# Turns by ordinary products, and the recurrence's transfers in quarters, in a two-block kernel on one core

## The chip, the cores and the metric

The kernel runs on one core of one Trainium2 chip. The metric is the device time of one execution in microseconds (us). Three timed runs of the kernel before gave 2231.57, 2232.23 and 2235.17 us, median 2232.23.

## The reference, cut to what matters

Two transformer blocks run one after the other on x of 256 tokens by 2048 channels, in float32: first windowed attention with a pooling branch and a gated feed-forward, then an RWKV-7 mixer followed by differential attention. The change lies in the RWKV-7 mixer of the second block. Its recurrence, with 32 heads of 64 channels:

```python
def step(S, inp):
    r_t, w_t, k_t, v_t, kk_t, a_t = inp
    sa = jnp.einsum('bhvk,bhk->bhv', S, kk_t)
    S = (S * w_t[:, :, None, :]
         - sa[..., None] * (kk_t * a_t)[:, :, None, :]
         + v_t[..., None] * k_t[:, :, None, :])
    y = jnp.einsum('bhvk,bhk->bhv', S, r_t)
    return S, y
...
mu = jnp.mean(y, -1, keepdims=True)
yc = y - mu
var = jnp.mean(yc * yc, -1, keepdims=True)
y = (yc * lax.rsqrt(var + GN_EPS)).reshape(B, T, C) * gn_g + gn_b
bonus = jnp.sum(rh * kh * r_k, -1, keepdims=True) * vh
y = (y + bonus.reshape(B, T, C)).astype(x.dtype)
return (y * jax.nn.silu(g)) @ w_out
```

## The kernel before, in words

Most of the time goes to large weight products. A unit of weights is 512 KB; SyncE loads it (`raw_w`), ScalarE makes its high part (`w_hi`), VectorE the low part (`w_lo`), and TensorE multiplies. All instructions stand in an order written out by hand, engine by engine, and semaphores tie the engines together.

The recurrence (called WKV here) is done in chunks of 64 tokens: `STEPS` has 16 steps n = (group g of 8 heads, chunk c), four steps to a group, and from 1505 to 1624 us the program does little else. In step n TensorE does, in this order: `x_second` (the state's part of X), `k_pairs(n + 1)`, a product with the inverse (`u_done` rises to 2n + 1), `turn_v(n + 1)`, the cross product, `beta_pairs(n + 1)`, the state's part of the output, the second product with the inverse (`u_done` 2n + 2), `turn_k(n + 1)`, the product that updates the state, `turn_beta(n + 1)`, `x_first(n + 1)` and the output (`y_done` n + 1). Between them ScalarE and VectorE copy what the next product needs: `XS` (L1898), `US` (L1902), the second copies of U (ScalarE L1908, VectorE L2575), K and beta turned (L1880), the state's two steps (L2587, L2589, or L2593 alone when c is 0). The turns of k and beta belong to steps whose next step has c < 3; where the step itself has c = 3 there is no state update, and `x_first` comes ahead of `turn_beta`.

A turn brings a 128 x 64 tile into token order by the identity, four tiles at a time. `turn_v` (L1247) uses ordinary products that write partitions 0 to 63 and 64 to 127 in turns. `turn` (L1249 to L1256) uses a product (L1253) where the output lies in partitions 64 to 127 and TensorE's transpose mode (L1255) where it lies in 0 to 63. An ordinary float32 product shows as two instructions in the trace, a transpose as one.

SyncE issues every transfer. Before the steps it issues three `load_t` and the eight broadcasts of the bonus rows (`spread_bonus`, 256 KB each). Then, for each n from 3 on, it waits for `y_done` n - 2 and issues `load_t(n)` (the inverse blocks and cross blocks of step n, in eight small transfers, three buffers deep); at eight of these places `first_unit`, a 512 KB unit of the weights that follow; and at three of them `spread_rows`, which waits for a group's rsqrt rows, stores them, waits for the store and loads them back broadcast (`GWIDE`, two transfers of 256 KB). `head_pair` on VectorE uses `GWIDE` and the bonus; GpSimd multiplies the bonus by v (`times_v`). At c = 0 of groups 1 to 3 VectorE also makes the reciprocal of the variances (L2611), and in groups 2 and 3 a `head_pair` behind it. On ScalarE, steps 5, 9 and 13 end with a Sqrt of the rows (in step 5 behind a table load) and the split of a weight unit, ahead of the next step's `XS`.

Of the kernel before, what the change touches and what calls it, by code (L numbers as in the profile page):

```python
# [14 lines left out]
P = 128  # L15
T = 256
# [126 lines left out]
def program(nc, h):  # L143
# [14 lines left out]
    with root:  # L158
# [291 lines left out]
        lt_dram, t_dram, x_dram = dram("lt_scratch", (P, 3, H, H)), dram("t_scratch", (P, 2, H, H)), dram("x_scratch", (P, KD, T))  # L450
# [47 lines left out]
        def _(sp):  # L498
# [66 lines left out]
            def load_t(n):  # L565
                g, c = STEPS[n]
                m = n % 3
                src = t_dram.rearrange("(f c h) b s t -> c h b s f t", c=NCH, h=2)
                for hh in range(2):
                    for b in range(2):  # L570
                        at = 64 * hh + H * b
                        sp.dma_start(TB[at:at + H, m, :, H * b:H * b + H], src[c, hh, b, :, 4 * g:4 * g + 4, :])\
                          .then_inc(t_loaded[m], 16)
                cross = lt_dram.rearrange("(f c h) b s t -> c h b s f t", c=NCH, h=2)
                for e in range(2):
                    for h_ in range(2):
                        sp.dma_start(CRS[64 * (1 - e):64 * (1 - e) + H, m, 2 * h_:2 * h_ + 2, H:], cross[c, h_ ^ e, 2, :, 4 * g + e:4 * g + 4:2, :])\
                          .then_inc(t_loaded[m], 16)


            def store_lt(f):
                sp.wait_ge(lt_ready, f + 1)
                dst = lt_dram[8 * f:8 * f + 8].rearrange("(c h) b s t -> h b s c t", h=2)
                for hh in range(2):
                    for b in range(2):
                        at = 64 * hh + H * b
                        sp.dma_start(dst[hh ^ f % 2, b], (XS, US)[f % 2][at:at + H, :, H * b:H * b + H]).then_inc(lt_stored[f % 2], 16)
                    sp.dma_start(dst[hh ^ f % 2, 2], (XS, US)[f % 2][64 * hh:64 * hh + H, :, H:]).then_inc(lt_stored[f % 2], 16)
# [25 lines left out]
            for n in range(NW):  # L614
# [7 lines left out]
                if n == 71:  # L622
                    for even_odd in lt_stored:
                        sp.wait_ge(even_odd, 96 * KD // 2)
                    sp.dma_start(LT[:, :, :, :], lt_dram[:, 0:2]).then_inc(inv_in, 16)
# [12 lines left out]
            def first_unit(n, w):  # L638
                sp.wait_ge(unit_done, seen(unit_done))
                sp.dma_start(RAWW[:, n, :, :], w.rearrange("(k p) n -> p k n", p=P)[:, n // 2 * KU:(n // 2 + 1) * KU,  # L640
                                                                                   n % 2 * UNIT_COLS:(n % 2 + 1) * UNIT_COLS])\
                  .then_inc(landed[n], 16)

            def spread_bonus(g):

                for h_ in range(2):
                    sp.dma_start(BON[64 * h_:64 * h_ + 64, 4 * g:4 * g + 4, :], b_dram[2 * g + h_:2 * g + h_ + 1].broadcast_to([64, 4, T]))\
                      .then_inc(bon_in, 16)

            def spread_rows(g):  # L650

                sp.wait_ge(gn_rstd, g + 1)
                for i in range(4):
                    sp.dma_start(g_dram[g, :, i, :], GROWS[32 * i:32 * i + 2, 1, :]).then_inc(gn_stored, 16)
                sp.wait_ge(gn_stored, 64 * (g + 1))
                if g:
                    sp.wait_ge(gn_out, 2 * g)
                for h_ in range(2):
                    sp.dma_start(GWIDE[64 * h_:64 * h_ + 64, :, :], g_dram[g, h_:h_ + 1].broadcast_to([64, 4, T])).then_inc(gn_loaded, 16)
# [15 lines left out]
            sp.wait_ge(gn_loaded, 96)  # L675
# [23 lines left out]
        def _(pool):  # L699
# [45 lines left out]
            def times_v(g):  # L745
                pool.wait_ge(bon_in, 128)
# [8 lines left out]
            def step(n):  # L755
# [10 lines left out]
                if n in (3, 5, 7, 9):  # L766
                    times_v((n - 3) // 2)
# [16 lines left out]
        def _(pe):  # L784
# [521 lines left out]
            def step(n):  # L1306
# [9 lines left out]
                pe.wait_ge(t_loaded[n % 3], 128 * (n // 3 + 1))  # L1316
# [126 lines left out]
        def _(act):  # L1443
# [5 lines left out]
            def split_unit(u, ku=KU):  # L1449
                act.wait_ge(landed[u], seen(landed[u], 16))  # L1450
# [434 lines left out]
            def head_rstd(g):  # L1885
                act.wait_ge(gn_var, g + 1)
                if g:
                    act.wait_ge(gn_loaded, 32 * g)
# [6 lines left out]
            def step(n):  # L1895
# [18 lines left out]
                if n in SPLIT_AT:  # L1914
                    split_unit(SPLIT_AT.index(n))
# [10 lines left out]
            split_unit(4)  # L1926
            head_rstd(3)
            split_unit(5)
            split_unit(6)
            for p_ in (6, 7):  # L1930
                act.wait_ge(gn_gated, p_ + 1)
                act.activation(C4H[:, 2 * p_:2 * p_ + 2, :], BET[:, 2 * p_:2 * p_ + 2, :], ACT.Copy).then_inc(gn_hi, 1)
                if p_ == 6:
                    split_unit(7)
# [129 lines left out]
        def _(dve):  # L2064
# [502 lines left out]
            def step(n):  # L2567
# [37 lines left out]
                if c == 3 and 0 < g < 3:  # L2605
                    dve.wait_ge(gn_loaded, 32 * g)
# [32 lines left out]
            dve.wait_ge(gn_loaded, 96)  # L2639
# [248 lines left out]
```

## Time and profile before

| | |
|---|---|
| timed runs | 2231.57, 2232.23, 2235.17 us |
| profiled execution, own time | 2236.7 us |
| its span | 2234.9 us |
| granted TensorE clock, mean | 0.991 |
| busy: TensorE, its weight loads, VectorE, ScalarE, GpSimd | 98%, 83%, 67%, 48%, 4% |
| chain that ended last | TensorE 88%, VectorE 8%, ScalarE 2%, issue 2% |
| mean traffic | 172 GB/s |

The table says that TensorE sets the time nearly everywhere. Busy shares are means over stages, so what a change inside the recurrence is worth has to be read from that stretch: 1505 to 1624 us, where many small products follow one another through copies on the other engines. "Issue" is time in which an engine waited for nothing that the profile shows. A timeline row gives the start, the time from first start to last end of merged instructions, engine, line, operation and count, and in brackets the idle time before with its releaser.

### The profile page before, as it was taken

To read this page: it belongs to the slowest core of one execution; us is meant where nothing else is said; L and a number is where in the kernel's file an instruction comes from. 1 tells how busy PE (TensorE), PEld (TensorE's weight loads), DVE (VectorE), ACT (ScalarE), POOL (GpSimd) and SP (SyncE) were. 2 spreads that over 40 slices of the span, in tenths; PEclk is the share of its full clock that TensorE was granted. 3 is DMA by queue.
4 is the path that set the end of the run, shared out by engine and by line. 5 is a ranking of instruction groups with operands and counts; after the bars stand their busy time and mean duration, and the time that the engine had idled before them with its cause. 6 is when DMAs were issued, how large, how long until landed. Compare 5 with 4: busy or idle time off the path is not lost.

```text
span 2234.9 us, 38358 instructions
## 1 busy us (share of the span) xinstructions
PE 2183.0 (98%) x14672; PEld 1856.4 (83%) x14672; DVE 1486.2 (67%) x2054; ACT 1079.9 (48%) x1520; POOL 89.1 (4%) x78
## 2 busy tenths in 40 slices
PE   9999999999999999999899999998999999999997
PEld 7888888888888888888788888886688888888886
DVE  6656568885588856875884589764576644566655
ACT  5444564444444434445544756444434534456533
POOL 0700000000000000000000000001210000000000
PEclk9999999999999999999999999999999999999998
DMA  8654555665666666656465555652355555654562
GB/s 290 207 161 155 170 151 178 189 188 186 189 189 188 188 187 189 188 163 192 136 221 142 174 162 164 203 158 61 81 183 161 170 187 189 189 153 145 166 187 85
DMA packets 400097, 383.35 MB, mean 172 GB/s; under 512 B 44009, under 2 KB 397857, under 8 KB 399137
## 3 DMA queue, kind: packets, MB, share of 16 engines
q1 hardware_dynamic: 399970, 381.59, 55.5%
q8 instruction: 88, 1.44, 0.3%
q14 instruction: 39, 0.32, 0.0%
HBM read 374.65 MB, written 6.87 MB: 171 GB/s over the span
## 4 chain that ended last, share of the span: by engine, by line
PE 88%; DVE 8%; ACT 2%; issue 2%; DMA 1%; DVEq 0%; SPq 0%; ACTq 0%
PE acc L795 45%; PE acc L798 22%; PE acc L826 3%; PE acc L881 2%; PE acc L882 2%; PE acc L883 2%; PE aux L1167 2%; PE acc L829 2%; DVE w_lo L2076 2%; PE acc L1253 1%; ACT w_hi L1452 1%; PE aux L1076 1%; PE aux L898 1%; PE aux L1096 1%; PE acc L1255 0%
## 5 line engine op out<-in xcount | busy, mean ns | idle before, releaser
L2076 DVE TENSOR_TENSOR w_lo<-raw_w,w_hi 128x1024 fp32r<-128x1024 f32 (+1 forms) x592 | 712.9, 1224 | 456.4 <-ACT w_hi L1452 454.9
L1452 ACT ACTIVATE w_hi<-raw_w 128x1024 fp32r<-128x1024 f32 (+1 forms) x592 | 613.3, 1046 | 674.5 <-PE acc L798 575.0
L795 PE MATMUL acc<-h,w_hi 128*128 128x512 f32 x1664 | 525.8, 397 | 1.2 <-DVE w_lo L2076 1.2
L798 PEld LDWEIGHTS acc<-h,w_lo 128*128 128x128 f32 x1664 | 312.6, 188 | 73.8
L798 PE MATMUL acc<-h,w_lo 128*128 128x256 f32 x1664 | 327.0, 278 | 0.0
L795 PEld LDWEIGHTS acc<-h,w_hi 128*128 128x128 f32 x1664 | 254.5, 189 | 2.2 <-issue 1.4
L795 PE MATMUL acc<-x_split,w_hi 128*128 128x512 f32 x704 | 225.2, 401 | 0.0
L795 PE MATMUL acc<-ff,w_hi 128*128 128x512 f32 x704 | 221.7, 396 | 2.4 <-DVE ff L2333 2.4
L795 PE MATMUL acc<-xs_b,w_hi 128*128 128x512 f32 x512 | 162.5, 399 | 1.7 <-DVE w_lo L2521 0.9
L798 PEld LDWEIGHTS acc<-ff,w_lo 128*128 128x128 f32 x704 | 132.2, 188 | 31.2
L798 PEld LDWEIGHTS acc<-x_split,w_lo 128*128 128x128 f32 x704 | 132.2, 188 | 31.2
L795 PE MATMUL acc<-xs_a,w_hi 128*128 128x512 f32 x448 | 143.7, 402 | 3.2 <-DVE w_lo L2076 3.2
L2521 DVE TENSOR_TENSOR w_lo<-raw_w,w_hi 128x1024 fp32r<-128x1024 f32 x96 | 116.7, 1222 | 44.5 <-ACT w_hi L1831 43.2
L798 PE MATMUL acc<-x_split,w_lo 128*128 128x256 f32 x704 | 138.6, 278 | 0.0
L798 PE MATMUL acc<-ff,w_lo 128*128 128x256 f32 x704 | 138.3, 278 | 0.0
L1831 ACT ACTIVATE w_hi<-raw_w 128x1024 fp32r<-128x1024 f32 x96 | 100.5, 1053 | 54.9 <-PE acc L798 43.1
L798 PEld LDWEIGHTS acc<-xs_b,w_lo 128*128 128x128 f32 x512 | 96.2, 188 | 22.7
L795 PEld LDWEIGHTS acc<-x_split,w_hi 128*128 128x128 f32 x704 | 108.1, 189 | 4.1 <-issue 3.1
L795 PEld LDWEIGHTS acc<-ff,w_hi 128*128 128x128 f32 x704 | 107.1, 189 | 4.2 <-DVE ff L2333 2.0
L798 PEld LDWEIGHTS acc<-xs_a,w_lo 128*128 128x128 f32 x448 | 84.1, 188 | 19.9
L798 PE MATMUL acc<-xs_b,w_lo 128*128 128x256 f32 x512 | 100.7, 278 | 0.0
L1519 ACT ACTIVATE fold<-acc 128x512 f32<-128x512 f32 x128 | 74.7, 583 | 30.4 <-PE acc L798 20.5
(374 smaller groups left out, 3128.6 us busy)
## 6 DMA issues: line engine op xcount, KB each, us to landing
raw_w<-in_w_up SPq DMA_DIRECT2D x176, 512.0 KB, 3.5
raw_w<-in_a_w_in SPq DMA_DIRECT2D x128, 512.0 KB, 3.8
raw_w<-in_w_in SPq DMA_DIRECT2D x64, 512.0 KB, 4.0
raw_w<-in_w_down SPq DMA_DIRECT2D x64, 512.0 KB, 3.6
raw_w<-in_b_w_qg SPq DMA_DIRECT2D x64, 512.0 KB, 3.8
raw_w<-in_w_o SPq DMA_DIRECT2D x32, 512.0 KB, 3.6
raw_w<-in_a_w_out SPq DMA_DIRECT2D x32, 512.0 KB, 3.6
raw_w<-in_w_k_shared SPq DMA_DIRECT2D x32, 512.0 KB, 3.7
```

The source lines that it names most:

```text
L795: pe.matmul(ACC[2 * b + f], WHI[:, q, k, f * P:(f + 1) * P], op[:, kt, :, :].rearrange("p h t -> p (h t)"), start=first, stop=False)
L798: mm = pe.matmul(ACC[2 * b + f][:, 0:T], WLO[:, slot, k, f * P:(f + 1) * P], op[:, kt, 0, :], start=False, stop=last)
L826: pe.matmul(ACC[2 * b + f], WHI[:, (2 * x + b) % 4, k, f * P:(f + 1) * P], op[:, kt, :, :].rearrange("p h t -> p (h t)"), start=first, sto ...
L829: mm = pe.matmul(ACC[2 * b + f][:, 0:T], WLO[:, 2 * x + b, k, f * P:(f + 1) * P], op[:, kt, 0, :], start=False, stop=last)
L881: pe.matmul(out, xh, wh[:, :, k, :], start=(kt == 0), stop=False)
L882: pe.matmul(out, xh, wl[:, :, k, :], start=False, stop=False)
L883: mm = pe.matmul(out, xl, wh[:, :, k, :], start=False, stop=(kt == KD - 1))
L1452: act.activation(WHI[:, u % 4, 0:ku, :], RAWW[:, u, 0:ku, :], ACT.Copy).then_inc(hi_made, 1)
L1519: act.activation(FOLD[:, j0:j0 + 2, :], BANKS[:, j0:j0 + 2, T:], ACT.Copy, scale=scale).then_inc(low_half, 1)
L1831: act.activation(WHI[:, n % 4, :, :], RAWW[:, slot, :, :], ACT.Copy).then_inc(hi_made, 1)
L2076: dve.tensor_tensor(WLO[:, u, 0:ku, :], RAWW[:, u, 0:ku, :], WHI[:, u % 4, 0:ku, :].bitcast(F32), ALU.subtract)\
L2521: dve.tensor_tensor(WLO[:, slot_of(n), :, :], RAWW[:, slot_of(n), :, :], WHI[:, n % 4, :, :].bitcast(F32), ALU.subtract)\
```

## The change

All turns of k and beta become ordinary products, four in a row. SyncE's order in the recurrence is rewritten around three events of each step. Each step may carry one transfer of 512 KB (a weight unit, a bonus spread or the spread of the rsqrt rows), cut into four quarters of 128 KB: the first goes out when X of the step is done, the second and third at the two `u_done` events, the fourth behind `y_done` and `load_t`. The bonus broadcasts move from ahead of the steps into steps 0, 3, 5 and 8; the rows of groups 0 to 2 go in steps 6, 10 and 14; the weight units in the steps 1, 2, 4, 7, 9, 11, 12 and 13. The cross blocks get a scratch of their own (`cross_dram`), laid out so that `load_t` takes two transfers for them in place of four. GpSimd's `times_v` moves from steps 3, 5, 7, 9 to 2, 5, 7, 10. Counts of the semaphores follow.

```diff
+        cross_dram = dram("cross_scratch", (4, NCH, 2, H, 4, H))
...
-                for e in range(2):
-                    for h_ in range(2):
-                        sp.dma_start(CRS[64 * (1 - e):64 * (1 - e) + H, m, 2 * h_:2 * h_ + 2, H:], cross[c, h_ ^ e, 2, :, 4 * g + e:4 * g + 4:2, :])\
-                          .then_inc(t_loaded[m], 16)
+                for e in range(2):
+                    sp.dma_start(CRS[64 * (1 - e):64 * (1 - e) + H, m, :, H:], cross_dram[g, c, e]).then_inc(t_loaded[m], 16)
...
+            UNIT_AT, BONUS_AT, ROWS_AT = [1, 2, 4, 7, 9, 11, 12, 13], [0, 3, 5, 8], [6, 10, 14]
+            def unit_quarter(n, k):
+                if k == 0:
+                    sp.wait_ge(unit_done, seen(unit_done))
+                row, col = (n // 2 * KU + k) * P, n % 2 * UNIT_COLS
+                sp.dma_start(RAWW[:, n, k, :], h["a_w_out_2"][0, row:row + P, col:col + UNIT_COLS]).then_inc(landed[n], 16)
+            def bonus_quarter(g, k):
+                if k == 0 and g:
+                    sp.wait_ge(bon_in, 64 * g)
+                sp.dma_start(BON[32 * k:32 * k + 32, 4 * g:4 * g + 4, :], b_dram[2 * g + k // 2:2 * g + k // 2 + 1].broadcast_to([32, 4, T]))\
+                  .then_inc(bon_in, 16)
+            def rows_quarter(g, k):
+                if k == 0:
+                    sp.wait_ge(gn_rstd, g + 1)
+                    for i in range(4):
+                        sp.dma_start(g_dram[g, :, i, :], GROWS[32 * i:32 * i + 2, 1, :]).then_inc(gn_stored, 16)
+                    sp.wait_ge(gn_stored, 64 * (g + 1))
+                    if g:
+                        sp.wait_ge(gn_out, 2 * g)
+                sp.dma_start(GWIDE[32 * k:32 * k + 32, :, :], g_dram[g, k // 2:k // 2 + 1].broadcast_to([32, 4, T])).then_inc(gn_loaded, 16)
...
-            UNIT_AT = [4, 6, 8, 9, 10, 12, 13, 14]
-            for g in range(4):
-                spread_bonus(g)
-            for n in range(3, 4 * NCH):
-                sp.wait_ge(y_done, n - 2)
-                load_t(n)
-                if n in UNIT_AT:
-                    first_unit(UNIT_AT.index(n), h["a_w_out_2"][0])
-                if n >= 7 and n % 4 == 3:
-                    spread_rows(n // 4 - 1)
+            for s_ in range(4 * NCH):
+                sp.wait_ge(x_done, s_ + 1)
+                quarter(s_, 0)
+                sp.wait_ge(u_done, 2 * s_ + 1)
+                quarter(s_, 1)
+                sp.wait_ge(u_done, 2 * s_ + 2)
+                quarter(s_, 2)
+                if s_ + 3 < 4 * NCH:
+                    sp.wait_ge(y_done, s_ + 1)
+                    load_t(s_ + 3)
+                quarter(s_, 3)
...
-                if n in (3, 5, 7, 9):
-                    times_v((n - 3) // 2)
+                if n in (2, 5, 7, 10):
+                    times_v((2, 5, 7, 10).index(n))
...
             def turn(x, n, half):
                 for i in range(4):
-                    if half ^ i % 2:
-                        mm = pe.matmul(KB_BANK[64:P, i * P:(i + 1) * P], tile_of(x, n, i), IDENT, start=True, stop=True)
-                    else:
-                        mm = pe.transpose(KB_BANK[0:64, i * P:(i + 1) * P], tile_of(x, n, i), IDENT)
+                    b = half ^ i % 2
+                    mm = pe.matmul(KB_BANK[64 * b:64 * b + 64, i * P:(i + 1) * P], tile_of(x, n, i), IDENT, start=True, stop=True)
```

TensorE at steps 0 and 1, before. The names are the turned tile (`consts,x` is turn_v, `consts,k` turn_k, `consts,beta` turn_beta), `aux<-wkv_x,inverse_blocks` the product with the inverse, `acc<-wkv_small` the state's update.

```order
L1167 MATMUL aux<-wkv_x,inverse_blocks 64x64 x8
L1255 MATMUL acc<-consts,k 64x128
L1253 MATMUL acc<-consts,k 64x128
L1255 MATMUL acc<-consts,k 64x128
L1253 MATMUL acc<-consts,k 64x128
L1167 MATMUL acc<-wkv_small 64x64 x8
L1253 MATMUL acc<-consts,beta 64x128
L1255 MATMUL acc<-consts,beta 64x128
L1253 MATMUL acc<-consts,beta 64x128
L1255 MATMUL acc<-consts,beta 64x128
```

The same place now.

```order
L1256 MATMUL acc<-consts,x 64x128 x4
L1176 MATMUL aux<-wkv_u,cross_blocks 64x64 x8
L1243 MATMUL acc<-r_kappa,beta 64x64 x8
L1176 MATMUL aux<-wkv_x,inverse_blocks 64x64 x8
L1262 MATMUL acc<-consts,k 64x128 x4
L1176 MATMUL acc<-wkv_small 64x64 x8
L1262 MATMUL acc<-consts,beta 64x128 x4
```

Nothing changed place on TensorE; each turn is now one form of instruction, the one that turn_v (L1256 now) has.

SyncE's queue from the rows of group 0 to `load_t(10)` with the unit behind it, before. L654 stores the rsqrt rows, L659 spreads them, L572 and L577 are load_t, L640 the weight unit.

```order
L654 DMA head_rstd_scratch<-head_rstd_rows 2x256 x4
L659 DMA head_rstd_wide<-head_rstd_scratch 64x1024 x2
L572 DMA inverse_blocks<-t_scratch 32x4x32 x4
L577 DMA cross_blocks<-lt_scratch 32x2x32 x4
L640 DMA raw_w<-in_a_w_out 128x4x256
L572 DMA inverse_blocks<-t_scratch 32x4x32 x4
L577 DMA cross_blocks<-lt_scratch 32x2x32 x4
L640 DMA raw_w<-in_a_w_out 128x4x256
```

From the same rows, now in step 6 (L655 and L659), to `load_t(10)` and the unit's last quarter in step 7.

```order
L655 DMA head_rstd_scratch<-head_rstd_rows 2x256 x4
L659 DMA head_rstd_wide<-head_rstd_scratch 32x1024 x3
L573 DMA inverse_blocks<-t_scratch 32x4x32 x4
L576 DMA cross_blocks<-cross_scratch 32x4x32 x2
L659 DMA head_rstd_wide<-head_rstd_scratch 32x1024
L643 DMA raw_w<-in_a_w_out 128x256 x3
L573 DMA inverse_blocks<-t_scratch 32x4x32 x4
L576 DMA cross_blocks<-cross_scratch 32x4x32 x2
L643 DMA raw_w<-in_a_w_out 128x256
```

The rows' last quarter moved behind the six transfers of `load_t(9)`; `load_t(8)` no longer stands behind the rows; and the 512 KB in one piece are gone.

## Rows read from the trace of the kernel before

**Rows 1.** TensorE's timeline (start us, us, line, shapes, count), turns of step 5.
```profile
1544.49 0.66 PE L1247 MATMUL acc<-consts,x 128*64 128x128 f32 x8
1545.08 0.46 PE L1167 MATMUL aux<-wkv_u,cross_blocks 64*64 64x64 f32 x16
...
1546.09 0.46 PE L1167 MATMUL aux<-wkv_x,inverse_blocks 64*64 64x64 f32 x16
1546.48 0.30 PE L1255 MATMUL acc<-consts,k 128*64 128x128 f32 x1
1546.71 0.43 PE L1253 MATMUL acc<-consts,k 128*64 128x128 f32 x2
1547.07 0.30 PE L1255 MATMUL acc<-consts,k 128*64 128x128 f32 x1
...
1548.04 0.38 PE L1253 MATMUL acc<-consts,beta 128*64 128x128 f32 x2
...
1549.17 1.08 PE L1167 MATMUL aux<-wkv_small 64*64 64x64 f32 x32
```

**Rows 2.** TensorE's timeline, the same stretch of step 14, without turns.
```profile
1615.98 0.46 PE L1167 MATMUL aux<-wkv_x,inverse_blocks 64*64 64x64 f32 x16
1616.99 0.69 PE L1167 MATMUL acc<-wkv_small 128*64 128x64 f32 x16 [0.55 <-DVE wkv_small L2575]
1617.61 1.08 PE L1167 MATMUL aux<-wkv_small 64*64 64x64 f32 x32
```

**Rows 3.** TensorE's timeline, step 11 into step 12.
```profile
1594.45 0.46 PE L1167 MATMUL aux<-wkv_x,inverse_blocks 64*64 64x64 f32 x16
...
1597.60 0.69 PE L1167 MATMUL aux<-wkv_small 128*64 128x64 f32 x16
...
1598.72 0.46 PE L1167 MATMUL aux<-wkv_x,inverse_blocks 64*64 64x64 f32 x16
```

**Rows 4.** Timeline of step 8, VectorE and TensorE.
```profile
1575.71 0.42 DVE L2593 TENSOR_TENSOR wkv_s<-acc,chunk_decay 128x256 f32<-128x256 f32 x1 [0.47 <-PE acc L1167]
...
1579.23 0.88 DVE L2628 SCALAR_TENSOR_TENSOR beta<-beta,params,bonus 128x256 f32<-128x256 f32 x2
...
1580.50 0.46 PE L1234 MATMUL acc<-r_kappa,beta 64*64 64x64 f32 x16 [0.35 <-DVE wkv_small L2553]
```

**Rows 5.** Timeline of steps 6 to 8, TensorE and SyncE's queue.
```profile
1559.55 0.43 SPq L640 DMA_DIRECT2D raw_w<-in_a_w_out  x1
...
1561.91 0.46 PE L1167 MATMUL aux<-wkv_x,inverse_blocks 64*64 64x64 f32 x14
...
1564.83 0.37 PE L1167 MATMUL aux<-wkv_x,inverse_blocks 64*64 64x64 f32 x2 [2.46 <-issue]
...
1571.44 0.40 PE L1167 MATMUL aux<-wkv_x,inverse_blocks 64*64 64x64 f32 x16
```

**Rows 6.** DMA view, 1559 to 1564 us (packets, MB, share of 16 engines).
```profile
q8 instruction: 1, 0.02, 2.5%
...
raw_w<-in_a_w_out SPq DMA_DIRECT2D x1, 512.0 KB, 5.9
```

**Rows 7.** DMA view, whole execution.
```profile
q8 instruction: 88, 1.44, 0.3%
```

**Rows 8.** Windows: length, TensorE busy (instructions), granted clock, DMA share, GB/s.
```profile
1564.00:1565.00 1.00, 0.17 (x2) 0.71 0.18 34
...
1622.00:1623.00 1.00, 0.45 (x20) 0.72 0.97 410
```

**Rows 9.** Timeline of step 3: SyncE's queue, TensorE, VectorE.
```profile
1529.43 1.73 SPq L572 DMA_DIRECT2D inverse_blocks<-t_scratch  x4
...
1532.50 0.46 PE L1167 MATMUL aux<-wkv_x,inverse_blocks 64*64 64x64 f32 x16
...
1533.48 0.69 DVE L2559 TENSOR_TENSOR wkv_small<-acc,consts 128x512 f32<-128x512 f32 x1
```

**Rows 10.** Tile view of the rsqrt rows' scratch.
```profile
DMA to landing us min/median/max: 3.4/4.0/4.9
```

More of the change, by code:

```diff
@@ L449, in by_chunk @@
             return x.rearrange("p (c t) -> p c t", c=NCH)
-        lt_dram, t_dram, x_dram = dram("lt_scratch", (P, 3, H, H)), dram("t_scratch", (P, 2, H, H)), dram("x_scratch", (P, KD, T))
+        cross_dram = dram("cross_scratch", (4, NCH, 2, H, 4, H))
+        lt_dram, t_dram, x_dram = dram("lt_scratch", (P, 2, H, H)), dram("t_scratch", (P, 2, H, H)), dram("x_scratch", (P, KD, T))
         g_dram, b_dram = dram("head_rstd_scratch", (3, 2, 4, T)), dram("bonus_scratch", (8, 4, T))
@@ L624, in _ @@
                         sp.wait_ge(even_odd, 96 * KD // 2)
-                    sp.dma_start(LT[:, :, :, :], lt_dram[:, 0:2]).then_inc(inv_in, 16)
+                    sp.dma_start(LT[:, :, :, :], lt_dram).then_inc(inv_in, 16)
                 if n == 84:
@@ L636, in _ @@
                 load_t(n)
[L638 to L659, printed above, removed]
@@ new lines, in quarter @@
+            def quarter(s_, k):
+                if s_ in UNIT_AT:
+                    unit_quarter(UNIT_AT.index(s_), k)
+                if s_ in BONUS_AT:
+                    bonus_quarter(BONUS_AT.index(s_), k)
+                if s_ in ROWS_AT:
+                    rows_quarter(ROWS_AT.index(s_), k)
+            sp.wait_ge(bon_stored, 64)
+            for s_ in range(4 * NCH):
[9 more added lines that the diff above has]
+                quarter(s_, 3)
@@ L674, in _ @@
             sp.wait_ge(tok_done, v_turned(4 * NCH - 1))
-            sp.wait_ge(gn_loaded, 96)
+            sp.wait_ge(gn_loaded, 192)
             sp.wait_ge(bon_done, KD)
@@ L745, in times_v @@
             def times_v(g):
-                pool.wait_ge(bon_in, 128)
+                pool.wait_ge(bon_in, 64 * (g + 1))
                 b4 = BON[:, 4 * g:4 * g + 4, :]
@@ L1315, in step @@
                     k_pairs(n + 1)
-                pe.wait_ge(t_loaded[n % 3], 128 * (n // 3 + 1))
+                pe.wait_ge(t_loaded[n % 3], 96 * (n // 3 + 1))
                 pe.wait_ge(xs_ready, n + 1)
@@ L1447, in _, with split_unit @@
             seen(acc_free, 4, "tile")
-            def split_unit(u, ku=KU):
-                act.wait_ge(landed[u], seen(landed[u], 16))
+            def split_unit(u, ku=KU, transfers=1):
+                act.wait_ge(landed[u], seen(landed[u], 16 * transfers))
                 act.wait_ge(unit_done, seen(unit_done))
@@ L1887, in head_rstd @@
                 if g:
-                    act.wait_ge(gn_loaded, 32 * g)
+                    act.wait_ge(gn_loaded, 64 * g)
                 act.activation(GROWS[:, 1, :], GROWS[:, 0, :], ACT.Sqrt).then_inc(gn_rstd, 1)
@@ L1914, in step @@
                 if n in SPLIT_AT:
-                    split_unit(SPLIT_AT.index(n))
+                    split_unit(SPLIT_AT.index(n), transfers=4)
             v_copies(0)
@@ L1925, in _ @@
             operand_hi(2)
-            split_unit(4)
+            split_unit(4, transfers=4)
             head_rstd(3)
-            split_unit(5)
-            split_unit(6)
+            split_unit(5, transfers=4)
+            split_unit(6, transfers=4)
             for p_ in (6, 7):
@@ L1933, in _ @@
                 if p_ == 6:
-                    split_unit(7)
+                    split_unit(7, transfers=4)
             def post_norm_gemm(which, bufs, more):
@@ L2605, in step @@
                 if c == 3 and 0 < g < 3:
-                    dve.wait_ge(gn_loaded, 32 * g)
+                    dve.wait_ge(gn_loaded, 64 * g)
                     head_pair(2 * (g - 1), [GWIDE[:, k, :] for k in range(2)])
@@ L2638, in _ @@
             operand_lo(1)
-            dve.wait_ge(gn_loaded, 96)
+            dve.wait_ge(gn_loaded, 192)
             head_pair(4, [GWIDE[:, k, :] for k in range(2)])
```

3 lines of the change are left out of this document (1 added, 2 removed).

## Prediction, made before the changed kernel was run

> **What bounds the kernel now.** I read the page's busy shares and chain first. TensorE is busy for nearly the whole span and carries 88% of the chain. That holds for the weight products, which the change leaves alone. So I went to the windows of the recurrence and then to the timelines of single steps there, engine by engine. The reader is to see three things.
>
> First, the turns. In step 5 [rows 1] four ordinary products of turn_v take 0.59 us from start to start of what follows (1544.49 to 1545.08). A turn of k is transpose, product, transpose, product: 0.23 us from a transpose to the product behind it, 0.36 from the product to the next transpose, so some 1.18 for four tiles. From the second product with the inverse (1546.09) to `x_first` (1549.17) step 5 needs 3.08 us. Step 14 has no turns [rows 2]: there the state's update starts 1.01 us behind the product with the inverse, because it waits for VectorE's copy of U, and `x_first` comes 0.62 behind that.
>
> Second, one long stop. In step 7 TensorE halts for 2.46 us between two products of one group of sixteen, with "issue" as the releaser [rows 5]: no semaphore, copy or DMA of the kernel is named, and the other fourteen products of the group, with the same waits behind them, had run. A 512 KB unit had been issued at 1559.55 and took 5.9 us to land; the only packet of TensorE's instruction queue in those 5 us took 2.5% of 16 engines, that is 2.0 us [rows 6], where the mean over the execution is 0.3% of 16 times 2235 us over 88 packets, 1.2 us [rows 7]. I read the stop as code that came late behind the weights.
>
> Third, the clock. It falls from 2.4 to 1.2 GHz at 1564.7, after that stop, and again at 1622.7, after two steps in which TensorE waited for copies (the windows show 0.71 and 0.72 as means [rows 8]). From the inverse's product in step 7 to the next in step 8 there are 9.53 us (1561.91 to 1571.44) [rows 5]; the same stretch of step 11 takes 4.27 (1594.45 to 1598.72) [rows 3]. The stop and the low clock together cost 5.26.
>
> **The turns.** 24 turns change form, two for each of 12 steps. I price a new turn at 0.59, the row of turn_v: same weights' shape (128 x 64), same moving columns, outputs in the two halves in turns.
> - Steps 0, 1, 4, 5, 9 and 13: the turn of k fits into the wait for U (0.39 for the inverse's product plus 0.59 is 0.98, under 1.01 [rows 2]), so the update starts at 1.01, the turn of beta at 1.63 and `x_first` at 2.22. Against 3.08 that is 0.86 each, 5.2 in all.
> - Steps 8 and 12: behind the state's update VectorE makes the state, the variance, a reciprocal and a `head_pair`, and only then reads kappa, for which TensorE already waited 0.35 us [rows 4]. From VectorE's L2593 to that product are 4.79 us and the turns don't shorten them. Only what lies ahead of the update counts: 1.95 (1546.09 to 1548.04 [rows 1]) less 1.63, that is 0.32 each, 0.6 in all.
> - Steps 3, 7 and 11: no update. `x_first` lies between the turns. 3.15 us (1594.45 to 1597.60 [rows 3]) become 1.01, 0.39 and 0.59, together 1.99: 1.16 each, 3.5 in all.
> - The two turns ahead of step 0 have nothing beside them; at the turn of beta's 1.13 in step 5 less 0.59 they give 1.1.
>
> Sum 10.4 us. What is late next? ScalarE's chain at the end of steps 5, 9 and 13 starts at the end of the turn of beta and moves with it. The state's two operations end 0.8 us ahead of their use, by the counts above, where there is a turn of beta to cover them.
>
> The Trainium skill speaks against this edit: Perfetto Trace Analysis, section Transposes, wants logical transposes made in transpose mode and not by a standard matmul. By the rule the new turn would cost more than the old; what that would give is a rival below, priced from rows. The trace disagrees with the rule for this shape as far as it goes: 0.59 for four products alone, 1.18 for the mixture.
>
> **The transfers.** From the first bonus spread on, SyncE's large issues go from 126 to 138: weights 8 to 32, bonus 8 to 16, rows 6 to 12, and thirteen `load_t` of six transfers in place of eight (104 to 78). A transfer of 16 KB costs 0.43 of SyncE's time (1.73 for four [rows 9]), so a `load_t` of six takes 2.6 us. `load_t(n)` is used three steps later (some 15 us) and hides fully; the units are used at steps 5, 9, 13, 14 and after, at least one step behind the last quarter; the bonus is multiplied two steps behind its issue. The three waits ahead of `load_t` are on events of the same step that TensorE raises before `y_done`, and the rows' wait for the Sqrt now stands in steps where it has just been made: nothing queues for long. These I cost at nothing. The cross blocks' stores keep their count and 128-byte rows, and are read some 50 units later; zero.
>
> The gain: with 128 KB at a time no burst like the one of 1559.55 stands ahead of the code. I take the stop and its low clock away: 5.3 us. The low stretches after other waits stay.
>
> The Trainium skill, Runtime: NRT & Kernel Launch, section Instruction fetch mechanics, has instructions refilled in 16 KiB blocks by the engine's own DMA queue, the crossing mostly hidden. The trace agrees on the size (88 packets, 1.44 MB [rows 7]) and not always on the hiding: 2.46 us in step 7. By the rule alone that stop would not be code, and the sum would be 5.3 less.
>
> The loss: the last quarter of the rsqrt rows stands behind `load_t`. Counted from `y_done` of step 6: 2.6 for `load_t`, then the landing. 256 KB took 3.4 to 4.9, median 4.0 [rows 10]; the trace has no such transfer of 128 KB. From below I take 16 KB like `load_t`'s at under 2 us, from above 4.9; I choose 3, so it lands at 5.6. `head_pair` is ready at 4.74 (1529.43 to the end of L2559 at 1534.17 in step 3 [rows 9]), so VectorE waits 0.9 us. `head_pair` takes two pairs like the 0.88 of L2628 [rows 4], the read of kappa 0.42 more: 7.7. TensorE wants kappa for `beta_pairs` at 3.07 (1529.43 to 1532.50 [rows 9]) plus 3.1 (4.27 less 1.16) plus the inverse's product, turn_v and the cross product, 1.3: 7.5. Loss 0.2 to 0.3, at two places (groups 0 and 1): 0.5. Ends: 0 and 2 us each, 4 in all. For group 2 the rows are used after the steps, with 5 us to spare.
>
> Sum on the profiled execution: 2236.7 - 10.4 - 5.3 + 0.5 = 2221.5. That execution lies 4.5 above the median of the runs, 2232.23. If the profile costs that much, the median after is 2217; if the runs at the median simply had no stop (their spread of 3.6 us allows it), it is 2232.2 - 10.4 + 0.5, or 2222.3. I take 2219, between the two.
>
> **Rivals.**
> - *The stop stays, or was never in the timed runs.* For: the profiled execution is above all timed ones, and pieces of 128 KB now move in almost every step, so one is more often there when code is fetched. Against: the code's packet was slow just behind the one large burst. Time: 2232.2 - 10.4 + 0.5 = 2222, with a stop of another size up to 2225.
> - *Low clock.* TensorE waits about as long as before per step while working less, so a larger share of each step is waiting. Each low stretch costs up to 9.53 - 4.27 - 2.46 = 2.8 us. Two more of them: 2219 + 5.6 = 2225. Against: turns that are gone leave no new gap, since the wait for U is only just uncovered by 0.03.
> - *The rows land late* and VectorE holds TensorE in steps 8 and 12 by the upper ends, and a landing above 4.9 adds more. At 7 us of landing: 4 us each, 8 in all, 2219 + 7.5 = 2227 to 2229, within the bound of no change.
> - *Products are the dear part of the turn.* If 0.36 (a product behind a transpose [rows 1]) is the price of a product with the identity and not of changing between modes, a turn costs 1.44 against 1.18, and 24 of them lose 6.2 us, with no cover. Without a gain from the transfers the time is 2238, slower. It decides from 0.30 us per product on. Against it: 0.15 per product in turn_v.
>
> **How the numbers follow.** Forecast as summed 0.68; the stop stays or wasn't there 0.17; low clock 0.07; rows late 0.05; dear products 0.03. No change means within 0.2%, 4.5 us, about what a measurement can tell. The first three lie below 2227.8: faster 0.92; the fourth gives same 0.05, the fifth slower 0.03. The range goes from 2213 (forecast by the profile's offset, with a further low stretch gone and no wait for rows) to 2226.
>
> **What would show it.** Right: one form in the turns' rows, four products in 0.6 us; 2.2 us from the inverse's product to `x_first` in steps 1, 4, 5, 9 and 13; TensorE's wait for kappa in steps 8 and 12 at 0.9 in place of 0.35; no "issue" of over 1 us on TensorE inside the steps; the steps' stretch shorter by 15 us; VectorE waiting about 1 us for the rows in steps 7 and 11. Wrong: products of the turns spaced by 0.3 or more; a stop with "issue" elsewhere in the steps; low clock over more than two stretches; `head_pair` released by a DMA after 2 us or more.

## The result: no gain, and slightly slower

| kernel | median of the runs, us | ratio to before, 95% |
|---|---|---|
| before | 2231.72 (2229.36 to 2235.3, 20 runs) | |
| after | 2234.71 (2231.26 to 2238.74, 20 runs) | 1.0015 (1.0008 to 1.0022) |

The forecast was 2219 us, 2213 to 2226. The loss of 3 us is real by its interval and smaller than the 0.2% that the prediction calls no change. The profiled execution of after took 2237.29 us (span 2235.5, TensorE's mean clock 0.988 against 0.991).

I call "stage" the stretch from the end of TensorE's wait for `silu_g`, ahead of step 0, to the first product with `wkv_out`. It took 118.7 us before (1505.31 to 1624.04) and 116.7 after (1506.97 to 1623.71). Inside it the times from one step's first product with the inverse to the next step's tell more: steps 0, 1, 3 and 5 became 1.0 us shorter each, step 7 6.4 us shorter (11.52 to 5.11), step 6 1.0 us longer, step 8 5.7 us longer (7.27 to 12.98) and step 12 7.05 us longer (7.33 to 14.38).

TensorE's timeline of step 5 in after (start us, us, line, shapes, count); it answers to [rows 1]:

```profile
1542.77 0.46 PE L1176 MATMUL aux<-wkv_x,inverse_blocks 64*64 64x64 f32 x16
1543.16 0.66 PE L1262 MATMUL acc<-consts,k 128*64 128x128 f32 x8
1543.78 0.69 PE L1176 MATMUL acc<-wkv_small 128*64 128x64 f32 x16
1544.30 0.61 PE L1262 MATMUL acc<-consts,beta 128*64 128x128 f32 x8
1544.84 1.08 PE L1176 MATMUL aux<-wkv_small 64*64 64x64 f32 x32
```

The turn of k is one row of eight records (a product of float32 has two, as the `L1253 ... x2` of the rows before), 0.62 us from its start to the update (1543.16 to 1543.78), and the turn of beta takes 0.54 (1544.30 to 1544.84). From the product with the inverse (1542.77) to `x_first` (1544.84) are 2.07 us, where the row before had 3.08 and the prediction 2.22.

Then SyncE's queue, VectorE, GpSimd and TensorE of after from step 6 into step 8, from the timeline; the releaser and its idle time stand in brackets. These rows answer to [rows 4, 5]:

```profile
1553.63 1.76 PE L1176 MATMUL aux<-wkv_small 64*64 64x64 f32 x32
...
1556.00 1.24 SPq L659 DMA_DIRECT2D head_rstd_wide<-head_rstd_scratch  x3
...
1557.28 1.85 SPq L573 DMA_DIRECT2D inverse_blocks<-t_scratch  x4
...
1559.17 1.93 SPq L576 DMA_DIRECT2D cross_blocks<-cross_scratch  x2
...
1561.15 0.59 SPq L659 DMA_DIRECT2D head_rstd_wide<-head_rstd_scratch  x1
...
1563.75 0.88 DVE L2630 SCALAR_TENSOR_TENSOR beta<-beta,params,head_rstd_wide 128x256 f32<-128x256 f32 x2 [3.46 <-DMA head_rstd_wide<-head_rstd_scratch]
...
1565.94 0.46 PE L1243 MATMUL acc<-r_kappa,beta 64*64 64x64 f32 x16 [2.77 <-DVE wkv_small L2560]
...
1567.61 1.08 PE L1278 MATMUL aux<-group_norm_squares,consts 128*32 128x128 f32 x16 [1.22 <-POOL group_norm_squares L774]
```

The first row is the group behind which `y_done` of step 6 is raised, at 1555.39. VectorE comes to the rows at 1560.29 and waits 3.46 us for the last quarter, which SyncE issued at 1561.15, behind the six transfers of `load_t(9)` (1557.28 to 1561.10). TensorE, by then in its step 8, waits 2.77 us for the kappa that VectorE makes next, and 1.22 more for GpSimd's squares, which hang on the same VectorE. Four steps later it is worse; the same kinds of rows from step 10 on, `y_done` at 1585.92:

```profile
1584.84 1.08 PE L1176 MATMUL aux<-wkv_small 64*64 64x64 f32 x32
...
1587.24 1.23 SPq L659 DMA_DIRECT2D head_rstd_wide<-head_rstd_scratch  x3
...
1588.52 2.69 SPq L573 DMA_DIRECT2D inverse_blocks<-t_scratch  x4
...
1591.25 2.33 SPq L576 DMA_DIRECT2D cross_blocks<-cross_scratch  x2
...
1593.63 0.59 SPq L659 DMA_DIRECT2D head_rstd_wide<-head_rstd_scratch  x1
...
1596.21 0.88 DVE L2630 SCALAR_TENSOR_TENSOR beta<-beta,params,head_rstd_wide 128x256 f32<-128x256 f32 x2 [5.48 <-DMA head_rstd_wide<-head_rstd_scratch]
...
1598.39 0.70 PE L1243 MATMUL acc<-r_kappa,beta 64*64 64x64 f32 x16 [4.78 <-DVE wkv_small L2560]
```

`load_t(13)` took 5.1 us of the queue instead of 2.6, and VectorE waited 5.48. The tile view of the wide rows in after, whose landing answers to [rows 10]:

```profile
L659 SPq DMA_DIRECT2D head_rstd_wide<-head_rstd_scratch x12: 307/421/937, 1556.0 to 1616.7; - x12
...
DMA to landing us min/median/max: 2.3/2.7/3.2
```

A quarter of the rows lands in 2.3 to 3.2 us, so the landing isn't what is late. Windows of after (length, TensorE busy and instructions, granted clock, DMA share, GB/s) show what followed:

```profile
1550.00:1560.00 10.00, 9.46 (x254) 0.68 0.37 86
1560.00:1570.00 10.00, 6.02 (x143) 0.84 0.40 107
1570.00:1580.00 10.00, 9.84 (x252) 0.82 0.19 49
1590.00:1600.00 10.00, 4.32 (x114) 0.87 0.31 75
1600.00:1610.00 10.00, 9.23 (x224) 0.79 0.27 67
```

A mean under 1 is a mixture of the two levels, 2.4 and 1.2 GHz. In the kernel with the turns alone (below) each of the five windows of 10 us from 1550 to 1600 has 1.00. The last four windows here hold the two waits and what came behind them. The first, 0.68, stands ahead of both: step 6 took 8.0 us at that clock, and 5.8 in a second profile of the same kernel.

### The profile page after: what moved, and what is told of

It reads as the page before. It is cut to its first block, busy times and chain, and to the rows that moved or that the text cites. A ratio compares the mean times of both kernels' runs of the same rounds, so it can differ in the third digit from the quotient of the medians.

```text
span 2235.5 us, 38477 instructions
## 1 busy us (share of the span) xinstructions
PE 2175.6 (97%) x14720; PEld 1858.2 (83%) x14720; DVE 1486.5 (66%) x2054; ACT 1079.8 (48%) x1520; POOL 89.5 (4%) x78
## 4 chain that ended last, share of the span: by engine, by line
PE 85%; DVE 9%; issue 2%; ACT 2%; DMA 1%; SPq 1%; POOL 0%; DVEq 0%; ACTq 0%; POOLq 0%
PE acc L804 45%; PE acc L807 22%; PE acc L835 3%; PE acc L890 2%; PE acc L891 2%; PE acc L892 2%; DVE w_lo L2083 2%; PE acc L838 1%; PE aux L1176 1%; PE aux L907 1%; PE aux L1085 1%; ACT w_hi L1459 1%; DVE w_lo L2528 1%; DVE inverse L2519 1%; DVE outer L2516 1%
## 5 line engine op out<-in xcount | busy, mean ns | idle before, releaser
L807 PEld LDWEIGHTS acc<-ff,w_lo 128*128 128x128 f32 x704 | 132.9, 189 | 31.5
L2528 DVE TENSOR_TENSOR w_lo<-raw_w,w_hi 128x1024 fp32r<-128x1024 f32 x96 | 116.7, 1222 | 43.0 <-ACT w_hi L1838 41.6
```

Source lines behind the costliest of these rows:

```text
L807: mm = pe.matmul(ACC[2 * b + f][:, 0:T], WLO[:, slot, k, f * P:(f + 1) * P], op[:, kt, 0, :], start=False, stop=last)
L2528: dve.tensor_tensor(WLO[:, slot_of(n), :, :], RAWW[:, slot_of(n), :, :], WHI[:, n % 4, :, :].bitcast(F32), ALU.subtract)\
```

## Experiments

Each kernel ran in rounds beside before on the same chip, and its ratio, with the interval in brackets, is to those runs of before. The first table is of one chip. In the second the first two kernels ran on another chip (before there 2232.42 us) and the last two on a third (before 2231.24), so a difference of two medians from different chips can be 1 us off. "Stage" and waits are of the one profiled execution, which can lie some us from its kernel's median.

### The two halves of the change apart, and two ways to be earlier

*Turns alone* is before with

```diff
-                    if half ^ i % 2: mm = pe.matmul(...)
-                    else: mm = pe.transpose(...)
+                    b = half ^ i % 2
+                    mm = pe.matmul(KB_BANK[64 * b:64 * b + 64, i * P:(i + 1) * P], tile_of(x, n, i), IDENT, start=True, stop=True)
```

> Only the turns become ordinary products; SyncE's order is the old one. Theory A (SyncE's queue is what lost the gain: in the changed kernel its issues fill 49 of 51 us from step 1 to step 8, so the rows' last quarter is issued late and VectorE waits 3.5 and 5.5 us): without the new order the turns bring their 10 us, so 2221 to 2223 us, and VectorE waits for no transfer of the rows. Rival B (turns by products don't pay, and the steps are held by something else, such as the copies on the other engines): 2229 to 2233 us.

*Transfers alone* is after with the old `turn`.

> Only the new order of the transfers; turns are mixed as before. Theory A: slower than before, 2236 to 2240 us, VectorE waiting for the rows in step 7 and 11 by 2 to 5 us in all steps (somewhat less than in the changed kernel, since steps are longer and SyncE has more time). Rival B: if the turns are at fault, this one is at or below the time of before, 2226 to 2232 us.

*Rows first* is after with the rows' last quarter ahead of `load_t`:

```diff
-                if s_ in ROWS_AT:
+                if s_ in ROWS_AT and k < 3:
                     rows_quarter(ROWS_AT.index(s_), k)
+                    if k == 2:
+                        rows_quarter(ROWS_AT.index(s_), 3)
```

> The changed kernel, with the last quarter of the rsqrt rows issued behind the third, ahead of load_t. Theory A: the quarter is issued 4 to 5 us earlier, VectorE waits less than 1 us in steps 7 and 11, the low clock that follows the stops goes as well, and the time falls by 12 to 14 us to 2221 to 2223. Rival C (the landing is slow because 128 KB pieces and load_t share the DMA engines, wherever the quarter stands): VectorE's wait stays above 2 us and the time above 2230.

*Bonus ahead* is after with `BONUS_AT = []` and the bonus in eight transfers ahead of the steps.

> The changed kernel, with the bonus spread ahead of the steps in eight transfers as before; SyncE issues 16 quarters less within steps 0 to 8. The last quarter of the rows still stands behind load_t. Theory A with a queue that runs late: in step 7 VectorE's wait for the rows falls from 3.5 to about 1 us (what the order alone costs, as predicted), in step 11, which has no bonus quarter near it, it stays at 5 us; time 2229 to 2232. Rival D (the order alone, no lateness of the queue): both waits stay, 2233 to 2235.

| kernel | median, us | ratio | stage, us | VectorE's waits for the rows, us |
|---|---|---|---|---|
| before | 2231.81 (23 runs) | | | |
| turns alone | 2222.17 (5 runs) | 0.9957 (0.9944 to 0.9970) | 104.5 | none |
| transfers alone | 2239.46 (6) | 1.0038 (1.0025 to 1.0051) | 120.4 | 5.9 in 2 |
| rows first | 2226.68 (11) | 0.9972 (0.9964 to 0.9981) | 106.3 | 1.0 in 1 |
| bonus ahead | 2230.66 (12) | 0.9998 (0.9989 to 1.0007) | 111.9 | 6.6 in 2 |

The turns gain 9.6 us where the sum had 10.4. All of the loss is in the transfers: 7.7 us with the old turns, 12.5 with the new ones (2234.71 less 2222.17). The shorter steps leave the rows less time: VectorE waits 8.9 us for them in after and 5.9 with the old turns. Moving one transfer of 128 KB per step with rows ahead of `load_t` gives 8.0 of the 12.5 back, less than I had expected of it. (Its stage of 106.3 us is of an execution of 2222.93 us, the fastest of its eleven, and looks better than the median.) With the bonus out of the queue the wait of step 7 falls to 1.6 us and that of step 11 stays at 5.0; 4 us come back. The longest stop of TensorE with "issue" in the steps of these profiles is 1.3 us, in step 0 of the turns alone.

### Is it the number of transfers, or their place?

*Whole, rows ahead* is after with a unit as one transfer at the step's first event, bonus and rows as two, the rows at the third event:

```diff
+                if k == 0: sp.dma_start(RAWW[:, n, :, :], h["a_w_out_2"][0]...(unit n whole)).then_inc(landed[n], 16)
...
+                if k == 2:
+                    for h_ in range(2):
+                        sp.dma_start(GWIDE[64 * h_:64 * h_ + 64, :, :], ...)
```

> The changed kernel with each step's 512 KB in one or two transfers instead of four: a unit as one at the step's first event, a bonus as two there, the rows as two behind the third event, ahead of load_t. The turns and the one-piece cross tiles stay. Theory A (the number of transfers that SyncE issues is the cost, about 0.6 us of its queue each): 24 of the units' transfers and 14 others go, 12 to 20 us of the queue, it is early again, no wait of VectorE for the rows is left, and the time is that of the turns alone, 2222 us, or up to 3 us better. Theory B (the places of the transfers, their bytes beside the steps' loads, cost the rest): it stays where the kernel with the rows' quarter ahead was, 2226 to 2228 us.

*Quarters at the old places* is the turns alone with each unit and each of the rows' loads in four transfers:

```diff
-                sp.dma_start(RAWW[:, n, :, :], ...)
+                for k in range(4):
+                    sp.dma_start(RAWW[:, n, k, :], ...)
```

> The turns by products with the transfers of the kernel before, at their old places behind load_t, cross tiles in four pieces, the bonus ahead of the steps, but each of the eight units and the three rows' transfers in quarters: 30 more transfers. Theory A (the number of transfers is the cost): the queue carries 15 to 18 us more in 100, the load_t behind a unit in quarters is late and TensorE waits for T or VectorE for the rows: 2227 to 2234 us. Theory B (only the place, the rows' last quarter behind a late load_t, is the cost; the number isn't): 2222 to 2224 us, no wait of VectorE for rows over 1 us.

*Whole, rows behind* is whole, rows ahead with `if k == 3` in place of `if k == 2` for the rows, that is, behind `load_t`.

> The changed kernel with each step's 512 KB in one or two transfers, and the two of the rows behind load_t, where the changed kernel has their last quarter. It is the fourth corner beside quarters behind (the changed kernel, 2234.7), quarters with the rows ahead (2226.7) and whole with the rows ahead (2224.2). Theory A (the number of transfers makes SyncE's queue late, and only a late queue makes the place behind load_t dear): 2223 to 2226 us, VectorE's waits for the rows under 2 us in all. Theory B (the place behind load_t costs by itself, whatever the number): 8 us more than with the rows ahead, 2231 to 2233, waits of VectorE for the rows of 6 to 9 us.

*Cross too* is the turns alone with `cross_dram`, so six transfers in `load_t`.

> The turns alone, and the cross tiles stored so that each step's come in two transfers instead of four (load_t issues six instead of eight), all else at its old place. Theory A: SyncE's queue waits for the events of the steps in the kernel with the turns alone (no late T there), so two transfers fewer buy nothing in the steps: 2221 to 2223 us. Theory B (late loads hold the steps, or the 12.9 us that SyncE waits is too little): 2218 to 2220 us. If the stores or the transfers of the new layout cost in themselves, it is slower than 2224 us.

| kernel | median, us | ratio | stage, us | waits, us |
|---|---|---|---|---|
| whole, rows ahead | 2224.2 (5) | 0.9964 (0.9950 to 0.9977) | 104.8 | none for the rows |
| quarters at the old places | 2225.3 (6) | 0.9969 (0.9957 to 0.9981) | 108.6 | TensorE for cross blocks, 4.0 in 2 |
| whole, rows behind | 2235.13 (11) | 1.0012 (1.0003 to 1.0021) | 116.5 | VectorE for the rows, 9.7 in 2 |
| cross too | 2222.01 (5) | 0.9953 (0.9940 to 0.9967) | 104.2 | none for the rows |

The first two came between what the two theories wanted. The third was the surprise, and my theory (the number of transfers makes the queue late, and only then the place is dear) fell by it: 24 fewer transfers for the units, and as slow as after. The timeline of whole, rows behind, steps 6 to 8:

```profile
1551.73 1.08 PE L1181 MATMUL aux<-wkv_small 64*64 64x64 f32 x32
...
1552.91 1.93 SPq L573 DMA_DIRECT2D inverse_blocks<-t_scratch  x4
...
1554.89 1.20 SPq L576 DMA_DIRECT2D cross_blocks<-cross_scratch  x2
...
1556.13 2.35 SPq L664 DMA_DIRECT2D head_rstd_wide<-head_rstd_scratch  x2
...
1562.26 0.88 DVE L2635 SCALAR_TENSOR_TENSOR beta<-beta,params,head_rstd_wide 128x256 f32<-128x256 f32 x2 [4.67 <-DMA head_rstd_wide<-head_rstd_scratch]
...
1564.44 0.71 PE L1248 MATMUL acc<-r_kappa,beta 64*64 64x64 f32 x16 [3.97 <-DVE wkv_small L2565]
```

and of whole, rows ahead:

```profile
1550.07 1.12 SPq L664 DMA_DIRECT2D head_rstd_wide<-head_rstd_scratch  x2
...
1552.53 2.85 SPq L573 DMA_DIRECT2D inverse_blocks<-t_scratch  x4
...
1557.19 0.87 DVE L2635 SCALAR_TENSOR_TENSOR beta<-beta,params,head_rstd_wide 128x256 f32<-128x256 f32 x2
```

In the first the queue was not late: SyncE stood in front of `load_t(9)` for `y_done` of step 6 (raised behind the first row, at 1552.81) and issued 0.1 us later; such waits make 31.5 us in 11 in that stage. `load_t` took 3.2 us, the rows' two issues 2.4, and the rows were there at 1562.26, 9.45 us behind the event. VectorE had come for them 4.78 us behind it. In the second they were issued at the third event of step 6, at 1550.07, and nobody waited at 1557.19. It is the moment: what stands behind `load_t` of step 6 can't be there for step 7's VectorE. By the ratios, each to its own chip's before, the one place costs 0.48%, 10.7 us. In before's order, which the turns alone keeps, the rows stood behind `load_t(7)`: there they left at 1548.78, ahead of `load_t(8)` and 4 us ahead of `y_done` of step 6 (1552.77), and cost nothing.

The number seems to have a price of its own, a smaller one. Quarters at the old places are 3.1 us slower than the turns alone by the medians, but the intervals of the two ratios overlap, and the 4.1 us by the stage are of an execution that lies 2.6 above its median (2227.94). What the trace does show is where such a price arises: TensorE waits for the last loads of a step (timeline of SyncE's queue and TensorE):

```profile
1585.21 3.26 SPq L642 DMA_DIRECT2D raw_w<-in_a_w_out  x4
...
1588.24 0.46 PE L1167 MATMUL aux<-wkv_x,inverse_blocks 64*64 64x64 f32 x16 [2.33 <-DMA cross_blocks<-lt_scratch]
```

One unit in quarters took 3.26 us of SyncE's queue here, where a whole one takes 0.43. Cross too shows that two fewer transfers in each `load_t` are worth nothing when the queue has time: 2222.01 against 2222.17. The turns alone and cross too are the fastest kernels of all that were run.

*One step earlier* is after with the rows' stores and quarters together behind `load_t` of the step before:

```diff
-                if s_ in ROWS_AT:
-                    rows_quarter(ROWS_AT.index(s_), k)
+                if k == 3 and s_ + 1 in ROWS_AT:
+                    for q in range(4):
+                        rows_quarter(ROWS_AT.index(s_ + 1), q)
```

> The changed kernel with the rows' stores and all four quarters together behind load_t of the step before (steps 5, 9 and 13 in place of 6, 10 and 14), all else as changed. After the whole transfers behind load_t had cost as much as the quarters, the number is no longer the theory. Theory C (the moment counts: y_done of step 6 comes 4.7 us ahead of VectorE's read, and load_t, the rows' issue and the landing need 8 to 10; one step earlier there are 7 us more): no wait of VectorE for the rows over 1 us, 2222 to 2227 us. Theory B (a place behind load_t is dear in itself): waits of 3 us and more stay, 2231 us or more.

It took 2225.57 us (9 runs), ratio 0.9970 (0.9959 to 0.9980), 9 us better than after, again behind a `load_t`. So the time came as theory C had it. The waits did not: VectorE still waited 4.9 us in 2, the longest 3.24. The timeline of steps 5 to 7 tells why:

```profile
1544.04 1.08 PE L1177 MATMUL aux<-wkv_small 64*64 64x64 f32 x32
...
1546.42 2.42 SPq L648 DMA_DIRECT2D bonus<-bonus_scratch  x3
...
1548.88 1.96 SPq L573 DMA_DIRECT2D inverse_blocks<-t_scratch  x4
...
1550.89 1.19 SPq L576 DMA_DIRECT2D cross_blocks<-cross_scratch  x2
...
1552.12 1.69 SPq L648 DMA_DIRECT2D bonus<-bonus_scratch  x1
...
1553.86 1.16 SPq L655 DMA_DIRECT2D head_rstd_scratch<-head_rstd_rows  x4
...
1556.22 2.04 SPq L659 DMA_DIRECT2D head_rstd_wide<-head_rstd_scratch  x4
...
1560.56 0.88 DVE L2631 SCALAR_TENSOR_TENSOR beta<-beta,params,head_rstd_wide 128x256 f32<-128x256 f32 x2 [3.24 <-DMA head_rstd_wide<-head_rstd_scratch]
```

Here the queue is late by its load. `y_done` of step 5 came at 1545.12, and `load_t(8)` was issued at 1548.88, 3.8 us later, behind three quarters of a bonus that took 2.42 us. From there on its only gap is the 1.2 us in which it waits for the stores to land, and the rows, due one `load_t` behind 1545.12, left at 1556.22. Place and number add up.

### Was the stop ever in the timed runs?

The kernel before twice more and the one after once more, unchanged, one profile each.

> The kernel before, unchanged, once more with a profile: whether the 2.46 us stop of TensorE's instructions in step 7, with the low clock behind it, is there in each execution or came by chance. If it is part of the program's course (theory A of the prediction), step 7 is 11.5 us long again and the stop stands at the same instructions within 1 us. If it came by chance, step 7 is some 9 us or less, and the stop is gone or elsewhere.

> The kernel before, unchanged, a third profile. The first had a 2.46 us stop of TensorE in step 7 and a stage of 118.7 us, the second had none and 113.8. If the stop is a chance of single executions, this one has the steps of the second (stage 113 to 115 us, execution 2231 to 2232 us), or a stop at another place; if there are two fixed courses, it is one of the two exactly.

> The changed kernel, unchanged, a second profile. If the late rows are part of its course, VectorE again waits 3 to 4 us and 5 to 6 us for them in steps 7 and 11 and the stage is 115 to 118 us; if they were a chance of the first profile, the waits are under 2 us and the stage under 110.

| execution | us | stage, us | step 7, us | longest "issue" stop in the steps, us |
|---|---|---|---|---|
| before, first profile | 2236.70 | 118.7 | 11.5 | 2.46 |
| before, second | 2231.75 | 113.8 | 6.35 | none |
| before, third | 2229.03 | 112.7 | 6.34 | none |
| after, first | 2237.29 | 116.7 | 5.1 | none |
| after, second | 2233.68 | 114.9 | 5.2 | none |

The stop is no part of the program's course: it stood in one of three executions of before. TensorE's timeline of the third execution, where [rows 5] had the stop, and SyncE's unit:

```profile
1559.92 0.43 SPq L640 DMA_DIRECT2D raw_w<-in_a_w_out  x1
...
1560.05 0.54 PE L1167 MATMUL aux<-wkv_x,inverse_blocks 64*64 64x64 f32 x16
...
1563.28 0.69 PE L1167 MATMUL aux<-wkv_small 128*64 128x64 f32 x16
...
1564.40 0.46 PE L1167 MATMUL aux<-wkv_x,inverse_blocks 64*64 64x64 f32 x16
```

The unit was issued at the same place in the order (1559.92) and nothing stopped: 4.35 us from the inverse's product of step 7 to that of step 8, where there had been 9.53. This unit took 3.5 us to land and the one instruction packet of those 5 us 1.2% of 16 engines, where [rows 6] had 5.9 and 2.5%. Both were slow together that once; which made which slow, or what made both slow, no run tells. The late rows are no chance: the second profile of after has VectorE waiting 9.1 us in 2 (longest 5.1), the first 8.9.

## Why the prediction was wrong

**The step that failed** is the loss: "the last quarter of the rsqrt rows stands behind `load_t`", costed at 0.5 with ends of 0 and 2 us each. The mechanism was named rightly and its size was far off: 8.0 us came back when the rows went ahead of `load_t`, and 12.5 is what the new order costs in all. Counted as there, in us from `y_done` (of step 6, and of step 10 in the last column):

| term | forecast | whole, rows behind | after, step 7 | after, step 11 |
|---|---|---|---|---|
| queue still busy | 0 | 0.1 | 1.9 | 2.6 |
| `load_t` | 2.6 | 3.2 | 3.9 | 5.1 |
| rows' issue and landing | 3 | 6.1 | 2.6 | 2.6 |
| rows are there | 5.6 | 9.45 | 8.4 | 10.3 |
| VectorE comes for them | 4.74 | 4.78 | 4.9 | 4.8 |
| wait | 0.9 | 4.67 | 3.46 | 5.48 |

The moment at which VectorE comes and the landing of a quarter (2.3 to 3.2 us, forecast 3) were right. Too small were `load_t`, priced at the fastest issue that [rows 9] show, and the queue's lateness, "nothing queues for long". In the 51.4 us from 1515.9 to 1567.3 SyncE was issuing for 48.7 us in after, against 37.2 before (37.5 in its third profile). I had compared 126 issues with 138. But before had its eight bonus transfers ahead of the steps, and the two cross transfers that are left take 0.60 each (1.19 for two), where the four small ones had taken 0.46 (1.84 for four). A count of the transfers in that window, 66 before and 81 in after, would have shown it, though only at a fair price: at the 0.43 of the prediction 81 of them are 35 us, at the 0.56 that before's window shows as a mean (37.2 over 66) they are 46 of 51.4.

**The second mistake** is what a wait costs behind VectorE. VectorE's wait of 3.46 us in step 7 became one of 2.77 for TensorE in its step 8; my cover of 0.7 was right. But 1.22 for GpSimd's squares came on top (0.45 in the turns alone, none in before), and then the low clock. Steps 8 and 12 were 12.4 us longer than in the turns alone (12.98 and 14.38 against 7.46 each) for 8.9 us of VectorE's waits; in whole, rows behind, 12.8 for 9.7. So each us of it cost about 1.3 to 1.4 on average. It is no fixed rate. VectorE's waits of 1.59 us (bonus ahead, step 7), 1.62 (one step earlier, step 11) and 2.18 (transfers alone, step 7) made TensorE's next step 1.7, 1.7 and 1.8 longer, with the granted clock at 1.00 throughout. In or behind each of the nine waits of 3.2 to 5.5 us the clock fell to 0.50 for some us, and the step grew by the wait and 1.4 to 2.3 more. Rows first does not fit: 0.97 us waited in step 11, a low clock behind it all the same, and 2.0 us lost. My rival "the rows land late" had step and order of size right, 8 us in all, and got 0.05; it was also reckoned at a landing of 7 us, the wrong term.

**The turns** came out: 9.6 us against 10.4. By steps, turns alone against the third profile of before: steps 1, 4, 5, 9 and 13 gave 1.0, 0.6, 1.0, 0.8 and 0.8 (forecast 0.86 each), steps 3, 7 and 11 gave 1.15, 1.2 and 0.8 (1.16 each), and 1.4 us went ahead of step 0 (1.1). Step 0 held the one stop of 1.3 us; in the other kernels with the new turns it gave its 1.0. Steps 8 and 12 lost 0.1 each where 0.32 was to be gained, the one part that fell: in step 8 of the turns alone TensorE waits 0.45 us for GpSimd's squares and 0.36 for VectorE's rows (`head_rstd_rows`), and in before neither wait is there. The rule of the Trainium skill against such products (Perfetto Trace Analysis, Transposes) doesn't hold here against the mixture of before: "dear products" would have lost 6 us. A turn of four transposes was never run, so whether it would be slower than four products stays open.

**The stop and the low clock**, 5.3 us, were read from one execution whose time stood 4.5 above the median of the runs. They were gone in two of three profiles of before too. (A finer window puts the fall of the clock at 1564.42, inside the stop, and not at 1564.7.) The prediction had seen both readings and took the mean of 2217 and 2222.3; the second, with the runs at the median as they are, is what the turns alone gave: 2222.2. That this is so close is in part luck, for the turns alone has neither the 0.5 of loss nor the full 10.4 of gain. The rule of the Trainium skill (Runtime: NRT & Kernel Launch, Instruction fetch mechanics) that the fetch is mostly hidden agrees with the four of these five executions that had no such stop; that the fifth's was a fetch is not shown.

**Sum against before:** turns -9.6; rows behind `load_t` of step 6 +8.0 (10.9 with whole transfers); the rest of the transfers +4.5, together +3. Of the 4.5, some 3 would be the quarters' own price, if what they cost at the old places holds here too, which no run shows. Between the forecast of 2219 and the 2234.7 measured lie 15.7 us: 12.0 are this loss (12.5 against 0.5), 3.3 the share of the stop that the forecast took as a gain (2222.3 less 2219), 0.8 the turns, and before itself came out 0.5 lower than its first three runs. What the spreading over the steps' events costs by itself stays open: rows first (2226.7) and whole, rows ahead (2224.2) have overlapping intervals, and so have the quarters at the old places and the turns alone.

## What to carry to other kernels

A transfer moved behind another in an in-order queue is priced by moments: when its predecessor's event comes, plus the predecessor's whole issue, plus its own and the landing, against the moment of its reader; here that is 8 to 10 us against 4.7. Before splitting transfers, add up the issue time that the queue then holds in each step, at the mean price that the busy stretch shows and not at the quickest, and compare it with the step. And a stall that a profile shows once, in an execution slower than the median of the runs, is no gain to be had until a second profile shows it again.

## What the hardware showed

- The time to issue a transfer isn't fixed. In the stage of after a `load_t`'s first four transfers took 1.75 to 3.20 us and its two cross transfers 1.19 to 2.33; in before the four took up to 3.88, beside the stop of step 7. Three quarters of a unit took 1.32 us at the quickest, and four took 3.26 at one place of the quarters at the old places. What makes them slow was not tested.
- Four products with the identity (128 x 64 weights) take 0.6 us, and 1.18 when every second one is in transpose mode [rows 1]; with its 24 turns changed so, the kernel is 9.6 us faster.
- The rows' quarters of 128 KB land in 2.3 to 3.2 us in after, median 2.7, and their halves of 256 KB in before in 3.4 to 4.9, median 4.0 [rows 10]: half the bytes land in two thirds of the time, and each piece has to be issued.
